# A two-layer diffusion backbone step: the order of the kernel's beginning and of the MoE router rewritten, norm sums spread over other work

## What is computed

```python
mod_p = (silu(c_ctx) @ w_ada[l] + b_ada[l])        # 6 x 1024 numbers for the context tokens
mod_s = (silu(c) @ w_ada[l] + b_ada[l])            # and for the latent tokens
h = rmsnorm(x, norm1) * (1 + sc1) + sh1
u = h @ w_in                                       # conv, Fourier, RWKV-7, merge gates
x = x + g1 * (merged @ w_o)
h = rmsnorm(x, norm2) * (1 + sc2) + sh2
x = x + g2 * ffn(h)      # layer 0: dense SwiGLU; layer 1: top-2-of-8 SwiGLU experts
# ffn of layer 1
logits = h @ w_router + b_router
top_v, top_i = top_k(logits, 2); top_p = softmax(top_v)
y += comb[:, e:e+1] * swiglu(h, w_gate[e], w_up[e], w_down[e])   # for each expert e
```

## Time and profile before

| | us |
|---|---|
| median of 3 runs | 1922.8 (1922.48 to 1926.27) |
| the profiled execution | 1924.78 |
| its span on the core | 1923.0 |
| TensorE busy | 1768.2 (92%) |
| ScalarE, VectorE, GpSimd busy | 906.2, 1133.0, 551.9 |
| granted TensorE clock, mean | 0.969 of full |

### The profile page before, as it was taken

How to read it: one execution, slowest core, us unless ns; L and a number is a source line. 1 busy time by engine, 2 the same in 40 slices (tenths; PEclk the granted TensorE clock), 3 DMA queues, 4 the chain that set the end, 5 groups by cost and what they waited for, 6 DMA issues and landing times.

```text
span 1923.0 us, 40900 instructions
## 1 busy us (share of the span) xinstructions
PE 1768.2 (92%) x16511; PEld 1620.0 (84%) x16511; DVE 1133.0 (59%) x1645; ACT 906.2 (47%) x1362; POOL 551.9 (29%) x417
## 2 busy tenths in 40 slices
PE   4997979899999999999988889999699999999996
PEld 3996868799999999989978788999588788888885
DVE  0465687755331121034666885632498898989888
ACT  2445232243443333333532414344367777777775
POOL 0571000165556666656500004565100000000000
PEclk8898999999999999989989999999799999999998
DMA  9447133233424444433562001342588999999880
GB/s 303 117 131 229 60 92 96 82 110 121 142 82 129 132 132 132 130 95 106 172 202 84 5 4 58 110 132 88 203 284 296 312 307 316 313 322 307 299 295 33
DMA packets 225173, 315.31 MB, mean 164 GB/s; under 512 B 15614, under 2 KB 169604, under 8 KB 224900
## 3 DMA queue, kind: packets, MB, share of 16 engines
q1 hardware_dynamic: 217856, 306.22, 49.1%
q10 hardware_dynamic: 7172, 6.97, 1.3%
HBM read 311.05 MB, written 2.10 MB: 163 GB/s over the span
## 4 chain that ended last, share of the span: by engine, by line
PE 77%; DVE 12%; issue 4%; ACT 3%; DMA 2%; ACTq 1%; DVEq 0%; SPq 0%; POOL 0%
PE bank L598 75%; PE bank L595 3%; DVE e_w_rest L186 2%; DMA ring<-in_w_ada 2%; DVE S L1918 2%; DVE cvT L1821 1%; ACT e_w_rounded L1609 1%; DVE hT L1700 1%; DVE hT L1694 1%; DVE hg_rest L1730 1%; DVE U L1948 1%; DVE St L1970 0%; DMA xin<-in_x_sample 0%; DVE St L1967 0%; DVE tmp L1836 0%
## 5 line engine op out<-in xcount | busy, mean ns | idle before, releaser
L2299 POOL TENSOR_TENSOR weights_rest<-ring,weights_rounded 128x512 fp32r<-128x512 f32 x344 | 467.7, 1362 | 450.5 <-ACT weights_rounded L1297 449.6
L186 DVE TENSOR_TENSOR e_w_rest<-e_raw,e_w_rounded 128x1024 fp32r<-128x1024 f32 (+1 forms) x327 | 354.9, 1132 | 34.0 <-ACT e_w_rounded L1609 33.0
L1297 ACT ACTIVATE weights_rounded<-ring 128x512 fp32r<-128x512 f32 x344 | 215.5, 629 | 330.5 <-PE bank L598 322.3
L1609 ACT ACTIVATE e_w_rounded<-e_raw 128x1024 fp32r<-128x1024 f32 (+1 forms) x327 | 314.7, 989 | 78.8 <-PE bank L598 77.2
L598 PE MATMUL bank<-h_rounded,weights_rounded 128*128 128x384 f32 x688 | 231.3, 336 | 5.5 <-POOL h_rest L2313 2.8
L598 PE MATMUL bank<-h_rounded,weights_rest 128*128 128x384 f32 x688 | 229.9, 334 | 0.0
L598 PE MATMUL bank<-h_rest,weights_rounded 128*128 128x384 f32 x688 | 229.9, 334 | 0.0
L598 PE MATMUL bank<-e_w_rounded,hG_rounded 128*128 128x512 f32 (+1 forms) x432 | 164.4, 381 | 6.2 <-DVE e_w_rest L186 6.2
L598 PE MATMUL bank<-e_w_rest,hG_rounded 128*128 128x512 f32 (+1 forms) x432 | 162.2, 376 | 0.0
L598 PE MATMUL bank<-e_w_rounded,hG_rest 128*128 128x512 f32 (+1 forms) x432 | 161.6, 374 | 0.0
L598 PEld LDWEIGHTS bank<-h_rounded,weights_rounded 128*128 128x128 f32 x688 | 129.1, 188 | 8.8 <-DVE h_rest L1730 4.1
(11 more groups left out here) (346 smaller groups left out, 3615.3 us busy)
## 6 DMA issues: line engine op xcount, KB each, us to landing
ring<-in_w_ada SPq DMA_DIRECT2D x96, 512.0 KB, 5.8
e_raw<-in_moe_w_down SPq DMA_DIRECT2D x90, 512.0 KB, 4.7
ring<-in_w_in SPq DMA_DIRECT2D x88, 512.0 KB, 4.8
e_raw<-in_moe_w_gate SPq DMA_DIRECT2D x72, 512.0 KB, 5.5
e_raw<-in_moe_w_up SPq DMA_DIRECT2D x72, 512.0 KB, 6.9
e_raw<-in_moe_w_gate SPq DMA_DIRECT2D x36, 384.0 KB, 3.9
e_raw<-in_moe_w_up SPq DMA_DIRECT2D x36, 384.0 KB, 4.0
ring<-in_ffn_w_gate SPq DMA_DIRECT2D x22, 512.0 KB, 4.9
```

Of the source, the lines that this page charges most:

```text
L186: eng.tensor_tensor(wl, e_raw[n % E_RAW][:, 0:kn * w], wr.bitcast(F32), ALU.subtract).then_inc(s("e_rest"), 1)
L1297: a(w_parts[n % NSLOT][0], raw, ACT.Copy).then_inc(*E.up("rounded_ready", *key))
L1609: a(e_w[n % E_PARTS][0][:, 0:kn * w], e_raw[n % E_RAW][:, 0:kn * w], ACT.Copy).then_inc(s("e_rounded"), 1)
L2299: pool.tensor_tensor(wl, raw, wr.bitcast(F32), ALU.subtract).then_inc(*E.up("rest_ready", *key))
```

## The change

**Beginning.** c and c_ctx are loaded into an own tile (`crow`) as the first two DMAs on ACT's queue, then the first table and x; the 15 vector loads of layer 0 are issued behind the sigmoid of c, those of layer 1 behind the squares, and the large table, the router's weights and the first states behind the modulation. The sigmoid's table is loaded before c is there. TensorE starts the w_ada halves as soon as `condp` is ready and does the transposes of x, the norm's sum, its row and the transposes of the vectors between the halves, with identity products behind most. DVE multiplies x by the norm's row before it has the modulation; all rests of h of this norm go to DVE, none to POOL. ACT rounds the second and the third piece of w_in between its modulations. The three loads of `low` move behind eight w_in blocks.

**Norm sums.** POOL adds the squares further: two more adds in the first norm of a layer's half (four summands left for TensorE), and five adds in the second norm (three summands left), two of the five between the rests of w_o. ACT squares the first six tiles inside the loop over w_o.

**Router.** wrt and brt are there from the beginning on. The transposes of x fill the waits of the norm. The logits are made by pairs of tiles of h, as each pair is modulated; their form (h as the moving operand) stays. The bias is added after the logits are turned. The rank takes 12 passes. The one-hot rows, slots and weights are made by fewer, wider DVE operations; the weights' part moves behind the job list. The gather takes the rounded part first. SP starts the experts' loads when the merged tiles' rests are done, for the first 14 of 18 buffers; the others wait for h as before. ACT rounds two pieces of expert weights around the norm's root, with the sigmoid's table loaded there too, and POOL makes the first piece's rest. DVE takes two of the six copies of `xtok`. The loop over experts itself is unchanged.

```diff
-                if key[0] == "z" and key[2:] == (0, 0):
+                if key[0] == "z" and key[2:] == (4, 0):
...
-            sp.wait_ge(*at("h2_ready", 1))
-            sp.wait_ge(*filled("o", 1, 7))
-            sp.wait_ge(*at("out_stored", "state", 1, 1))
+            sp.wait_ge(*at("x_parts", "merged", DEPTH - 1, 3))
...
+                    if job is None and n == BELOW_NORM:
+                        sp.wait_ge(*at("h2_ready", DEPTH - 1))
...
-                summands = [0, 2, 4, 6, 7]
+            def norm_total(l, which, meanwhile=None):
+
+                b = begin("norm", l, which, use=2 if (l, which) == (DEPTH - 1, 1) else None)
+                summands = (0, 6, 7) if which else (0, 4, 6, 7)
...
+                    if k == 0 and meanwhile:
+                        meanwhile()
...
-                    pe.wait_ge(*at("cond_ready"))
-                    for i in range(4):
-                        for _ in ada(0, i):
-                            pass
+                    pe.wait_ge(*at("first_in"))
+                    pe.wait_ge(*at("crow_in"))
+                    b = begin("cvec")
+                    transpose(b[:, 0:16], crow[0:16, :], 16).then_inc(*E.fill("cvec"))
+                    pe.wait_ge(*drained("cvec"))
+                    between = {0: lambda: filler(psum[7], 8), 1: lambda: filler(psum[7], 8), 2: x_transposes,
+                               3: lambda: filler(psum[7], 8), 4: lambda: norm_total(0, 0), 5: lambda: norm_row(0, 0, lambda: None),
+                               6: lambda: (vectors(0), vectors(1))}
+                    for n, _ in enumerate(half for i in range(4) for half in ada(0, i)):
+                        if n in between:
+                            between[n]()
+                        if n > 1:
+                            filler(psum[7], 4)
                     ada_turn(0, (0,))
+                    filler(psum[7], 16)
...
-                norm_sum(l, 0)
+                if l > 0:
+                    norm_sum(l, 0)
...
+            s = lambda name: sem(name).h
+            pe.sem_inc(s("e_used"), 2)
+
...
+            norm_total(DEPTH - 1, 1, lambda: (turn_x(0, 0), turn_x(1, 0)))
+            norm_row(DEPTH - 1, 1, lambda: turn_x(2, 0))
+            for j in range(3):
+                turn_x(j, 1)
+            pe.wait_ge(*at("router_in"))
+            logit = begin("logit", use=2)
+            filler(logit, 4)
+            for g in range(4):
+                pe.wait_ge(*at("h_odd", DEPTH - 1, 1, g))
+                pe.wait_ge(*h2_pair(g))
+                for k in (2 * g, 2 * g + 1):
+                    last = mm(logit[0:NE, 0:T], wrt[:, k, :], hT[:, k, :], k == 0, k == KD - 1)
+            last.then_inc(*E.fill("logit"))
+            pe.sem_inc(s("e_used"), E_PARTS - 2)
...
+            pe.wait_ge(*drained("norm_row", DEPTH - 1, 1))
+            filler(psum[3], 4)
+            b = begin("rank", use=2)
...
-            for j in range(3):
-                for i in range(j + 1):
-                    mm(b[:, j * NE:(j + 1) * NE], before if i == j else ones, ch[:, i * NE:(i + 1) * NE], i == 0, i == j)
+            mm(b[:, 0:24], before, ch, True, False)
+            mm(b[:, 8:24], ones, ch[:, 0:16], False, False)
+            mm(b[:, 16:24], ones, ch[:, 0:8], False, False)
             for i in range(3):
-                last = mm(b[:, 24:32], ones, ch[:, i * NE:(i + 1) * NE], i == 0, i == 2)
+                last = mm(b[:, 24:32], ones, ch[:, i * NE:(i + 1) * NE], False, i == 2)
...
+            for k in range(6):
+                pe.wait_ge(*at("htok_rounded", k))
             pe.wait_ge(s("e_sel"), 1)
+            for h in range(2):
+                gather(h, 0)
             for k in range(6):
                 pe.wait_ge(*drained("htok", k))
-            gather()
+            for h in range(2):
+                gather(h, 1)
...
+            for i, name in enumerate(("c_ctx", "c")):
+                act.dma_start(crow[8 * i:8 * i + 8, :], flat(dram[name]).rearrange("(r c) -> r c", c=P))\
+                    .then_inc(*E.up("crow_in", by=16))
             act.dma_start(first, dram["tables"][:, 0:n_first]).then_inc(*E.up("first_in", by=16))
+            for j in range(3):
+                src = dram["x_prompt"][0] if j == 0 else dram["x_sample"][0][(j - 1) * P:j * P, :]
+                act.dma_start(xin[:, j, :], src).then_inc(*E.up("x_in", by=16))
...
+            act.wait_ge(*at("zeroed", "stat"))
+            a(stat[:, 95:96], stat[:, 94:95], ACT.Sigmoid)
+            act.wait_ge(*filled("cvec"))
+            a(cond.rearrange("p k s -> p s k"), bank("cvec")[:, 0:16].rearrange("p (s k) -> p s k", s=2), ACT.Sigmoid)\
+                .then_inc(*E.up("cond_sig"))
+            rows_in(0)
...
+                squares(l)
                 if l == 0:
+                    rows_in(1)
+                    root(l, 0)
+                    vectors(0)
+                    vectors(1)
                     ada_copies(0, (0,))
-                start_phase(("z", l), ("cf", l))
-                root(l, 0)
-                act.wait_ge(*at("modA_ready", l, 0))
-                modulate(l, 0)
+                    allowed[:] = ("z", l), ("cf", l)
+                    convert(0)
+                    act.wait_ge(*at("modA_ready", l, 0))
+                    modulate(l, 0, between=convert)
+                    act.dma_start(second, dram["tables"][:, n_first:ncols]).then_inc(*E.up("second_in", by=16))
+                    act.dma_start(wrt, dram["w_router"][0].rearrange("(k p) e -> p k e", p=P)).then_inc(*E.up("router_in", by=16))
+                    act.dma_start(brt, dram["b_router"].broadcast_to([P, NE])).then_inc(*E.up("router_in", by=16))
+                    load_state(0)
+                else:
...
+                    if m in (3, 5, 7):
+                        i = (m - 3) // 2
+                        act.wait_ge(*drained("o", l, 2 * i + 1))
+                        square_pair(l, 1, i)
+                for m in (6, 7):
+                    act.wait_ge(*drained("o", l, m))
+                    square_one(l, 1, m)
                 if l % 2 == 0:
                     start_phase(("fg", l), ("fu", l), ("fd", l))
+                if l == DEPTH - 1:
+                    e_round(0, 0, 1)
                 root(l, 1)
+                if l == DEPTH - 1:
+                    a(stat[:, 95:96], eps[1e-6], ACT.Sigmoid)
+                    e_round(0, 1, 2)
...
+            act.wait_ge(*at("out_stored", "state", DEPTH - 1, 1))
+            e_round(0, 2, E_AHEAD)
+            round_tokens(range(2))
...
+                if meanwhile:
                     for g in range(4):
-                        tt(hT[:, 2 * g:2 * g + 2, :], xT[:, 2 * g:2 * g + 2, :],
...
+                        scaled_x(l, which, g)
+                    meanwhile()
+                for g in range(4):
+                    if not meanwhile:
+                        scaled_x(l, which, g)
+                    dve.wait_ge(*E.latest())
+                    k = 2 * g + 1
+                    for s_, (t0, t1) in enumerate(SEG):
+                        ins = ts(hT[:, k, t0:t1], hT[:, k, t0:t1], modAs[:, l, which, k, s_:s_ + 1],
+                                 mods[:, l, 24 * which + k, s_:s_ + 1], M, A)
+                    ins.then_inc(*E.up("h_odd", l, which, g))
+                    if meanwhile and g > 0:
+                        rest("z", l, g - 1, hT[:, 2 * g - 2:2 * g, :])
+                    elif g == 2 and (which == 0 or l % 2 == 0):
+                        rest("ffn" if which else "z", l, 1, hT[:, 2:4, :])
...
                     residual(lambda m: ("fdown", l, m), l, 40, 2)
 
+            dve.wait_ge(*filled("xtok", 2, 1))
+            dve.wait_ge(*drained("norm_row", DEPTH - 1, 1))
+            for half in range(2):
+                dve.tensor_copy(xtok[:, 2, half * 512:(half + 1) * 512], bank("xtok", 2, half)[:, :]).then_inc(*E.read("xtok", 2, half))
...
+            for i in range(2):
+                tt(group(R_OH + 24 * i, 3), code8.rearrange("p (j e) -> p j e", j=1).broadcast_to([P, 3, NE]),
+                   group(R_IF, 3)[:, :, i:i + 1].broadcast_to([P, 3, NE]), ALU.is_equal).then_inc(*E.step())
...
+            select_slots(lambda at_: slice(at_, at_ + 1)).then_inc(s("e_sel"), 1)
+            token_rests(range(1, 6))
...
+            pool.memset(stat[:, 94:95], 0.0).then_inc(*E.up("zeroed", "stat"))
             for l in range(DEPTH):
-                add_squares(l, 0)
+                for k, m in ((0, 1), (2, 3), (0, 2), (4, 5)):
+                    add_square(l, 0, k, m)
                 rests(("z", l), ("cf", l), count=NSLOT)
-                x_rests("z", l)
+                if l > 0:
+                    x_rests("z", l)
                 rests(("z", l), ("cf", l), first=NSLOT)
                 pool.wait_ge(*filled("cf", l, 5))
                 pool.memset(St, 0.0).then_inc(*E.up("St_zero", l))
```

365 lines of the change are left out of this document (167 added, 198 removed).

## The result

The changed kernel takes 1907.4 us (median of 6 runs, 1896.4 to 1913.5) where the kernel before, in the same comparison, takes 1924.5 (6 runs, 1920.8 to 1928.5): a ratio of 0.9897, 95% interval 0.9872 to 0.9923 (the two medians alone give 0.9911). That is faster, but by 17.2 us and not by 31.9, and 1907.4 lies above the range. Over all 16 runs the changed kernel's median is 1902.4, so the gain is nearer to 23 us; the size was still missed. The profiled execution took 1911.2 us, its span 1909.3, so 13.7 of the span were won in it.

The account below looks back on a forecast made before the run. TensorE holds 77% of the path, so time is won only in its waits or needless work. Start 12.5, second norms 1.1 and router 18.3 sum to 31.9: median 1922.8 to 1890.9 us, range 1883 to 1903.

Parts of the forecast that it names:

- The beginning, chain: Start: turn of w_ada at 40.7 instead of 46.98, last pair at 53.0 instead of 67.48, so 14.5 won.
- rival 2: Start held by TensorE's order: last landings 5 us later would leave 26.9 won, 1896; chance 0.12.
- which I price at 2.9 us by the issues of the trace, 0.36 to 0.8 each: Start: ACT's issues of second table, router loads and two states behind the modulation, with 1 us lost waiting for piece 3.
- The term of 12.5: Start: 14.5 won, less 1 us for piece 3's wait and 1 us for a clock below full.
- my lower bound of 7: Start: gain if the clock stays at half from 30 to 42 us, which takes 5.7 more.
- what is won at these points goes through to the end: Behind 67.48 and 1395.98 instructions stay as they are, apart from two second norms, so the gains reach the end.
- the side of 1903: Upper end of the forecast range for the median, 1883 to 1903 us.
- Layer 0's second norm: Sum with 18 passes instead of 30 ends at 557.3 instead of 558.47: 1.1 us won.
- 18.3 forecast: Router: 18.5 us won to the first expert product, taken as 18.3; bounds 13 and 20.
- To the logits' end: Router: no wait for the bias, logits by pairs end at 1362.2 instead of 1375.18, 13.0 won.
- rival 1: Clock stays at half at the start and in the router: 20.5 won, 1902.3; chance 0.13.
- Tables and transposes: Rules: a table cost 1.28, next operation but one 1.40 behind; whether transposes hold the clock was left unsettled.

Follow-up runs that it names:

- before_loads_early: The kernel before with only the router's weights and bias loaded early, in layer 0's feed-forward; 1920.8 us, ratio 0.9982 to the kernel before.
- experts_late: The changed kernel with the experts' first 18 transfers and first roundings held until the last modulation; last root to first expert's tokens 27.3 us, rest 532.0.
- before_again: The kernel before, unchanged, for a second trace; middle 1200.2 us with 56 us at half clock, router 43.3, rest 529.7.
- no_identities: The changed kernel without its new identity products at the beginning and in the router; square of the keys at 146.5 us, router 24.5.

## Why the prediction was wrong, point by point

**The beginning, chain.** Right to within 1 us: turn of w_ada at 40.85 (forecast 40.7), first w_in product 45.65 (46.3), last group 52.04 (53.0). 15.4 us were won to that point, and rival 2 did not come: TensorE's waits for w_ada fell to 2.0 us.

**The beginning, costs.** The step that failed is "which I price at 2.9 us by the issues of the trace, 0.36 to 0.8 each". The issues of that trace include the states right behind the table (0.71 and 0.83), but none stands behind the router's 1024 short rows and the table. Here the issue in that place took 2.4 to 4.9 us, and the five of the first trace 7.7 together. Piece 3's wait was 4.68 instead of 1, and the clock fell behind it. So of 15.4 only 7.7 were left at the square of the keys (86.1 us from the last group to there before, 93.8 after). The term of 12.5 measured 6.3 to 10.7 in three traces; with the bias first it is 11.9 to 14.9. The mechanism was right, the price of one issue wasn't. That two of the three lie above my lower bound of 7 is luck: the bound was drawn for the clock, and none of mine had an issue dearer than the single ones I had seen.

**The middle.** I held it fixed. One trace has it 8.4 longer, but 13 traces of changed kernels put it at 1 to 3 us. Taking "what is won at these points goes through to the end" from one trace was the second fault: the middle and the loop over experts took back some 2.6 us each, and my range had no term for either. It was no wider, 20 us, than the scatter between runs of one kernel. The same kernel's two later medians, 1902.2 and 1901.3, lie just inside it, so the side of 1903 was chance; that a third of the forecast gain was missing wasn't.

**Layer 0's second norm.** The changed kernel's timeline: the sum has 18 passes, the last six at 549.99, and the root comes 2.97 behind the sum's start instead of 3.44:

```profile
548.43 1.39 PE L598 MATMUL bank<-first,sq 128*128 128x1 f32 x12
...
549.84 1.66 ACT L1317 ACTIVATE weights_rounded<-ring 128x512 fp32r<-128x512 f32 x3
549.99 0.83 PE L598 MATMUL bank<-first,sq 128*128 128x1 f32 x6 [0.16 <-ACT sq L1284]
```

0.5 won instead of 1.1, and the last group of the first tile is 0.3 later (16.3 behind the sum's start, 15.9 before). The term is 0, not 1.1. The roundings on ScalarE were late next: they end at 551.50, and the root starts there, not at the sum's end (550.82). The 0.5 that was left went in the next step, the six passes of the row, which ran at a lower clock (0.66 from 550 to 555) than before (0.80 over them), first before and then after:

```profile
559.04 1.08 PE L598 MATMUL bank<-first,rs 128*128 128x128 f32 x6
...
551.91 1.65 PE L598 MATMUL bank<-first,rs 128*128 128x128 f32 x6 [0.26 <-DVE rs L1741]
```

**The router.** 18.3 forecast, 16.5 measured against the first trace of before and 19.2 against the second. To the logits' end 12.4 (22.6 - 10.2) of 13.0. Behind them the first product follows by 15.5 instead of 20.8: 5.3 of 5.5, of which 1.2 come from the first piece's rest, which GpSimd now makes, and 4.1 from the steps up to the tokens. Counted to the first product, as the forecast does, it is 17.7. The steps behind the logits came out by luck in part: the rank ended 4.5 behind them instead of the forecast 5.1, and what follows it took 11.0 instead of 10.2. The clock stayed up: passes of 0.34 (5.46 / 16), as by the earlier trace rows, so rival 1 is out in the router. At the start it holds in part, with 0.83 from 28 to 38.

**The rest.** Behind the router 2 to 3 us are lost in all new kernels, and in before_loads_early as well, whose loop is the old one. So it isn't the new loop order, nor fewer pieces landed (experts_late), nor the half clock (17 to 21 us in all). It is no single wait: between the same operations of the loop over experts, near 1450 and near 1873 us of before, the changed kernel falls behind evenly, 0.3 us in each 60, by 2.3 us in all. before_again keeps before's pace to 0.1 us. From 1460 to 1860 us the product's mean time shows it, 391 ns in before, 395 in the changed kernel and in before_loads_early, in this order:

```profile
L598 PE MATMUL bank<-e_w_rounded,hG_rest 128*128 128x512 f32 x236 | 92.3, 391 | 0.0
...
L598 PE MATMUL bank<-e_w_rounded,hG_rest 128*128 128x512 f32 x227 | 89.6, 395 | 0.0
...
L599 PE MATMUL bank<-e_w_rounded,hG_rest 128*128 128x512 f32 x233 | 91.9, 395 | 0.0
```

Why a product takes 1% longer was not found.

**The sum.** In the mean of three traces of the changed kernel and two of before: 8.3 at the start, 17.9 in the router, less 2.6 in the middle and 2.6 behind the router: 21.0 of 31.9. Missing are 4.2 at the start, 1.1 in the norm, 2.6 in the middle, 2.6 behind the router, and 0.4 in the router.

**Tables and transposes.** The sigmoid's table in the router cost 1.28, and the next two operations started 1.29 and 1.40 behind its start, in line with the earlier trace rows (1.28 and 1.40). On transposes the nearest run is no_identities, whose router keeps the full clock from 1351.9 to 1367.3 without identity products. But the sum's passes, the row and the logits stand between those transposes, so whether transposes hold the clock stays open.

## What to carry to other kernels

A DMA issue isn't priced by itself: here it took 0.24 to 1.2 us where the queue hadn't stalled, and 2.4 to 4.9 behind 1024 rows of 32 bytes that followed a 1696 KB load. Put such a load ahead of the large one or far from it, with no urgent work behind the two on the same engine, and look at the time of the issue behind them, not at their own. When one load's wait is removed, look for the buffer or bank that the waiting step needs next, because about half of the 12.4 us to the logits needed both changes. Compare two traces of each kernel before a difference in unchanged code is explained, and cut both at the same marks.
